# Projection to FFN: the last two units taken row block by row block, one normalisation factor per row block, constant products on TensorE, and the first chunk pair cast from a copy

## The reference, cut to what matters

```python
y = o.transpose(1, 0, 2, 3, 4).reshape(bn, n, d) @ w_o          # attention output projection
x = x + g1 * y                                                   # gated residual
hf = modulate(rms_norm(x, norm_ffn_g[i]), sh2, sc2)              # x * rsqrt(mean(x*x)+eps) * g, then (1+sc2), sh2
x = x + g2 * conv_ffn(hf, ffn_w_up[i], ffn_conv_w[i], ffn_conv_b[i], ffn_w_down[i])
```

## Time and profile before

| | |
|---|---|
| median of 3 runs | 2498.31 us (2495.0 to 2499.1) |
| profiled execution | 2497.54 us, span in the trace 2495.9 us |
| TensorE busy | 2469.8 us, 99% of the span |
| VectorE busy | 1788.2 us, 72% |
| ScalarE busy | 1185.5 us, 47% |
| GpSimd busy | 219.5 us, 9% |
| mean granted TensorE clock | 0.998 |

### The profile page before, as it was taken

How to read it: one execution, slowest core, us unless ns; L and a number is a source line. 1 busy time by engine, 2 the same in 40 slices (tenths; PEclk the granted TensorE clock), 3 DMA queues, 4 the chain that set the end, 5 groups by cost and what they waited for, 6 DMA issues and landing times.

```text
span 2495.9 us, 39539 instructions
## 1 busy us (share of the span) xinstructions
PE 2469.8 (99%) x14106; PEld 2157.8 (86%) x14106; DVE 1788.2 (72%) x2211; ACT 1185.5 (47%) x1517; POOL 219.5 (9%) x251
## 2 busy tenths in 40 slices
PE   9998999999999999999999999999999999999999
PEld 8988988888888888889999999988788888888887
DVE  6655766888898887787777777776666656665676
ACT  4445555544534535555333333344655435553463
POOL 5000000000000000222111111130200000000000
PEclk9999999999999999999999999999999999999999
DMA  8654586887787787775666656666566665566655
GB/s 269 182 133 110 153 282 204 273 298 243 258 275 247 240 288 246 251 221 167 198 188 186 195 183 198 185 217 191 179 188 193 193 194 178 185 198 194 185 176 173
DMA packets 279544, 519.07 MB, mean 208 GB/s; under 512 B 32750, under 2 KB 102648, under 8 KB 278672
## 3 DMA queue, kind: packets, MB, share of 16 engines
q1 hardware_dynamic: 254128, 403.66, 51.4%
q0 software_dynamic: 25120, 113.89, 14.7%
q10 hardware_dynamic: 192, 0.05, 0.0%
HBM read 515.35 MB, written 6.90 MB: 209 GB/s over the span
## 4 chain that ended last, share of the span: by engine, by line
PE 92%; DVE 3%; ACT 2%; DMA 2%; issue 1%; DVEq 0%; ACTq 0%
PE ps L1944 32%; PE ps L1971 22%; PE ps L1974 11%; PE ps L2452 7%; PE ps L2440 6%; PE ps L2445 4%; PE ps L1936 3%; PE ps L2394 1%; PE ps L2372 1%; DMA raw<-in_w_in 1%; DVE wlo L1199 1%; PE ps L2343 1%; DMA raw<-in_w_out 1%; PE ps L2261 1%; PE ps L2381 1%
## 5 line engine op out<-in xcount | busy, mean ns | idle before, releaser
L1199 DVE TENSOR_TENSOR wlo<-raw,whi 128x1024 fp32r<-128x1024 f32 (+1 forms) x776 | 943.9, 1228 | 424.0 <-ACT whi L706 407.3
L706 ACT ACTIVATE whi<-raw 128x1024 fp32r<-128x1024 f32 (+1 forms) x776 | 800.7, 1040 | 805.5 <-PE ps L1944 366.9
L1944 PE MATMUL ps<-whi,act 128*128 128x512 f32 (+3 forms) x2736 | 823.4, 382 | 1.9 <-DVE wlo L1199 1.2
L1971 PE MATMUL ps<-act,whi 128*128 128x512 f32 x2400 | 658.0, 395 | 1.7 <-DVE wlo L1199 1.4
L1944 PEld LDWEIGHTS ps<-whi,act 128*128 128x128 f32 x2736 | 505.4, 188 | 94.0 <-issue 3.2
L1944 PE MATMUL ps<-wlo,act 128*128 128x512 f32 (+3 forms) x1368 | 519.9, 380 | 0.0
L1971 PEld LDWEIGHTS ps<-act,whi 128*128 128x128 f32 x2400 | 410.2, 189 | 57.3 <-DVE wlo L1199 1.8
L1974 PEld LDWEIGHTS ps<-act,wlo 128*128 128x128 f32 x2400 | 369.5, 189 | 51.7
L1974 PE MATMUL ps<-act,wlo 128*128 128x256 f32 x2400 | 383.9, 281 | 0.0
L1944 PEld LDWEIGHTS ps<-wlo,act 128*128 128x128 f32 x1368 | 257.4, 188 | 45.0
L1525 DVE SCALAR_TENSOR_TENSOR arena<-arena,cond 128x768 f32<-128x768 f32 (+1 forms) x330 | 285.6, 888 | 5.9 <-DMA arena<-in_w_ada 2.6
(11 more groups left out here) (327 smaller groups left out, 2140.4 us busy)
## 6 DMA issues: line engine op xcount, KB each, us to landing
arena<-in_w_ada POOLq DMA_DIRECT2D x128, 768.0 KB, 5.8
raw<-in_ffn_w_up SPq DMA_DIRECT2D x160, 512.0 KB, 4.3
raw<-in_w_mlp_in SPq DMA_DIRECT2D x128, 512.0 KB, 4.8
raw<-in_w_mlp_out SPq DMA_DIRECT2D x128, 512.0 KB, 5.1
raw<-in_na_w_qkv SPq DMA_DIRECT2D x96, 512.0 KB, 4.8
raw<-in_ffn_w_down SPq DMA_DIRECT2D x84, 512.0 KB, 4.4
raw<-in_w_in SPq DMA_DIRECT2D x64, 384.0 KB, 3.7
raw<-in_w_in SPq DMA_DIRECT2D x32, 512.0 KB, 4.4
```

Of the source, the lines that this page charges most:

```text
L706: act.activation(a, b, ACT.Copy).then_inc(hi_done, 1)
L1199: dve.tensor_tensor(a, b, c, ALU.subtract).then_inc(lo_done, 1)
L1944: ins = pe.matmul(o, a, b, start=start and i == 0, stop=last and i == 2, skip_group_check=True)
L1971: pe.matmul(Z[q][:, c, :].rearrange("p (h t) -> p h t", h=2), kn(whi, j)[:, kk, P * c:P * c + P], act2[:, :, k, 0:S], start=k == 0, stop=k ...
```

## The change

On TensorE the last two units of the projection's last panel run together in `last_units`: first all products of row block 0 (which then counts up `wo_half`), then those of row block 1; both units are counted in `unit_used` at the end. VectorE adds row block 0, sums its squares, adds row block 1, squares it itself with a reducing product and sums again; ScalarE has one logarithm and exponential per row block, and all four scalings of row block 0 between the two. TensorE turns pairs 0 to 3 of row block 0 first, then issues four products of constants into `G[0]`, then turns row block 1. For pair 0 VectorE writes `turned_f` straight from the transposes, ScalarE casts `ahi` from that copy, and VectorE subtracts, chunk by chunk.

```diff
 ScalarE
-            for r in range(RT):
-                act.wait_ge(x4_ok, 4 + r)
-                own.done(act.activation(junk_w, x[:, r, 1536:D], ACT.Square, accum_out=psq[:, r, 3:4]))
+            act.wait_ge(x4_ok, 4)
+            own.done(act.activation(junk_w, x[:, 0, 1536:D], ACT.Square, accum_out=psq[:, 0, 3:4]))
             act.sem_inc(psq2_ok, 1)
-            act.wait_ge(mean_ok, 1)
-            own.done(act.activation(frms[:, 1, :], frms[:, 0, :], ACT.Ln, scale=1.0 / D, bias=EPS))
-            act.activation(frms[:, 1, :], frms[:, 1, :], ACT.Exp, scale=-0.5).then_inc(rms_ok, 1)
+            def row_rms(r):
+                act.wait_ge(mean_ok, r + 1)
+                own.done(act.activation(frms[:, 1, r:r + 1], frms[:, 0, r:r + 1], ACT.Ln, scale=1.0 / D, bias=EPS))
+                act.activation(frms[:, 1, r:r + 1], frms[:, 1, r:r + 1], ACT.Exp, scale=-0.5).then_inc(rms_ok, 1)
+            row_rms(0)
             act.wait_ge(rms_ok, 1)
+            for c in range(4):
+                scale_piece(c, xs, x, frms[:, 1, 0:1])
+            row_rms(1)
             act.wait_ge(coef_ok, 3)
...
-            scale_piece(0, xs, x, frms[:, 1, 0:1])
-            scale_piece(1, xs, x, frms[:, 1, 0:1])
-            turn(5, 0, g_ffn, b_ffn, at_=(0, 1))
-            scale_piece(2, xs, x, frms[:, 1, 0:1])
-            turn(5, 0, g_ffn, b_ffn, at_=(2,))
-            scale_piece(3, xs, x, frms[:, 1, 0:1])
-            turn(5, 0, g_ffn, b_ffn, at_=(3,))
+            for c in range(2):
+                act.wait_ge(a_f, 2 * KC + c + 1)
+                act.activation(ahi[:, c, 0:S], turned_f[:, 0, c, :], ACT.Copy).then_inc(a_hi, 1)
+            turn(5, 0, g_ffn, b_ffn, at_=range(1, 4))
             split(U_FFN, 3)
 VectorE
-            def turn(e, off, gain, shift=None, order=range(8), at_=range(8)):
+            def turn(e, off, gain, shift=None, order=range(8), at_=range(8), early=False):
                 for at in at_:
-                    dve.wait_ge(a_hi, TURN_AT[e] + 2 * at + 2)
+                    if early:
+                        dve.wait_ge(turned, 8 * e + at + 1)
+                    else:
+                        dve.wait_ge(a_hi, TURN_AT[e] + 2 * at + 2)
...
+            def add_last_row(r, ready):
+                dve.wait_ge(*ready)
+                v, y = x[:, r, 1536:D], tmp[:, 512 * r:512 * r + 512]
+                own.done(dve.tensor_tensor(y, G[1][:, r, :], gb[:, 1536:D], ALU.mult))
+                dve.tensor_tensor(v, v, y, ALU.add).then_inc(x4_ok, 1)
+            def row_mean(r):
+                dve.tensor_reduce(frms[:, 0, r:r + 1], psq[:, r, :], AXX, ALU.add).then_inc(mean_ok, 1)
...
-            add_last(1, U_WO + 32, drained[1])
+            add_last_row(0, (wo_half, 1))
             dve.wait_ge(psq2_ok, 1)
-            dve.tensor_reduce(frms[:, 0, :], psq[:, :, :], AXX, ALU.add).then_inc(mean_ok, 1)
-            dve.wait_ge(rms_ok, 1)
+            row_mean(0)
+            add_last_row(1, (unit_used, U_WO + 32))
+            dve.sem_inc(drained[1], 1)
+            dve.wait_ge(x4_ok, 5)
+            own.done(dve.tensor_tensor_reduce(tmp[:, 0:512], x[:, 1, 1536:D], x[:, 1, 1536:D], 1.0, 0.0, ALU.mult, ALU.add,
+                                              psq[:, 1, 3:4]))
+            row_mean(1)
+            dve.wait_ge(rms_ok, 2)
...
-            turn(5, 0, g_ffn, b_ffn, at_=(0,))
-            dve.wait_ge(a_f, 2 * KC + 2)
-            dve.tensor_tensor(alo[:, 0:2, 0:S], turned_f[:, 0], f(ahi[:, 0:2, 0:S]), ALU.subtract).then_inc(a_lo, 2)
+            turn(5, 0, g_ffn, b_ffn, at_=(0,), early=True)
+            for c in range(2):
+                dve.wait_ge(a_hi, TURN_AT[5] + c + 1)
+                dve.tensor_tensor(alo[:, c, 0:S], turned_f[:, 0, c, :], f(ahi[:, c, 0:S]), ALU.subtract).then_inc(a_lo, 1)
             turn(5, 0, g_ffn, b_ffn, at_=(1,))
 TensorE
-            def last_units(u0, parts, acc, t0, final):
+            def last_units(u0, parts, acc, t0, final, half):
                 pe.wait_ge(lo_done, u0 + parts[-1][0] + 1)
                 for r in range(RT):
...
                     if r == 0:
-                        ins.then_inc(half_rows, 1)
+                        ins.then_inc(half, 1)
                 ins.then_inc(unit_used, len(parts))
...
+                    if n == 3 and j >= 6:
+                        if j == 7:
+                            last_units(U_WO, ((30, 12, 2), (31, 14, 2)), G[1], S, KC - 1, wo_half)
+                        continue
                     unit_rows(U_WO, 8 * n + j, q, 2 * j, S)
...
+            def ffn_first_steps():
+                for r, scaled in enumerate((xs_a, xs_v)):
+                    for at in range(4):
+                        pe.wait_ge(scaled, 4 + at // 2 + 1)
+                        for c in range(2):
+                            k = 2 * at + c
+                            ins = pe.transpose(X[at][:, c * S + P * r:c * S + P * r + P], xs[:, r, P * k:P * k + P], ident)
+                        if r == 1:
+                            ins.then_inc(turned, 1)
+                    if r == 0:
+                        for _ in range(4):
+                            pe.matmul(G[0][:, 0, 0:S], ident, cst[:, 0:S], start=True, stop=True)
...
-                                ffn_steps(((0, 1, 2, 3), (4,), (5,), (6, 7))[j])
+                                if j == 0:
+                                    ffn_first_steps()
+                                else:
+                                    ffn_steps(((4,), (5,), (6, 7))[j - 1])
```

More of the change, by code:

```diff
@@ L344, in program @@
         xs_a, xs_v = sem("xs_a"), sem("xs_v")
-        x4_ok, psq2_ok, mean_ok, rms_ok = (sem("ffn_" + n) for n in ("x", "sq", "mean", "rms"))
+        x4_ok, psq2_ok, mean_ok, rms_ok, wo_half = (sem("ffn_" + n) for n in ("x", "sq", "mean", "rms", "half_rows"))
         hid_a, hid_v = sem("hid_a"), sem("hid_v")
@@ L2528, in _ @@
                         if j == 5:
-                            last_units(U_DOWN, ((21, 6, 2), (22, 8, 2), (23, 10, 1)), GD[1], S, 10)
+                            last_units(U_DOWN, ((21, 6, 2), (22, 8, 2), (23, 10, 1)), GD[1], S, 10, half_rows)
                     else:
```

## The result

The changed kernel takes 2501.23 us in the median of 22 runs, the kernel before 2497.28 us in 22 runs beside them (the three runs shown ahead had 2498.31).

The account below looks back on a forecast made before the run. TensorE, busy 2469.8 of 2495.9 us, bounds the kernel; only its 9.09 us seam between projection and FFN counts. FFN shift 4.1 plus stall 0.1 makes 4.2 us on 2497.54: 2501.7 us, range 2498.0 to 2505.0.

Parts of the forecast that it names:

- Head start: Row block 0, done 2.72 us ahead, gains nothing: unit 34's split waits ahead of it; its scaling comes 1.11 us later.
- Constant products: Four float32 products on TensorE ahead of row block 1's transposes: end at 1772.7, last 2.2 us on the path.
- The bounds: On TensorE, the constant products take 1.71 us at the upper clock, 3.41 us at the lower.
- case C: Constant products on TensorE cost nothing: FFN's first product 2.1 us later than before, time 2499.6 us; chance 0.09.
- Pair 0: Between transposes and the FFN's first product, pair 0 itself is faster by 1.6 us than the old way.
- Unit 1: In the FFN, TensorE may wait for GpSimd's low part of pair 1: 0 to 0.9 us, by the median 0.1.
- Slow start: FFN's first four products took 1.33 us instead of 1.09 before; starting at full clock takes 0.24 off the shift.
- A: TensorE's clock returns late, slowing constant products and pair 0's transposes: 5.2 to 5.3 us in all, 2502.8 us; chance 0.30.
- B: Row block 0's early finish is real, unit 34's split released at 1759.15: -0.4 to +1.8 us, 2497.1 to 2499.3; chance 0.06.

Follow-up runs that it names:

- units in order: Changed kernel with the projection's last two units run unit by unit, each counted at its end: ratio 1.0011 to the kernel before, seam 10.28 us.
- old pair 0: Changed kernel with pair 0 of the FFN's input made as in the kernel before: one execution only, no ratio, seam 13.67 us.
- each unit counted: Changed kernel with unit 30 counted behind its own last product, order and work unchanged: ratio 1.0014 to the kernel before, seam 11.88 us.
- eight products: Changed kernel with eight constant products instead of four: one execution only, no ratio, seam 15.38 us.
- no products: Changed kernel without its four constant products: ratio 1.0021 to the kernel before, seam 11.47 us.
- shortened seam: Changed kernel with unit 34's split moved behind the second logarithm (ScalarE) and ahead of the FFN's next split (VectorE): ratio 0.9994; also without constant products, 1.0001.

## Why the prediction was right

2501.7 us was forecast with 4.2 us more than the profile before; the seam grew by 4.23, and the median by 4 us. The mechanism was right in both costs, the late split and the uncovered products. That the seam is met to 0.03 us is luck: it hangs on the clock's return, which came 4.37 us after the first transpose as in the kernel before, but after 2.9 to 5.0 in the experiments that kept the products and a late first transpose, and that moves the seam by up to 0.75 us.

**Head start.** Lost as forecast, by the split of unit 34. Gate product forecast 2.37 behind the projection's end, found 2.34; first transposes 6.17 forecast and found. Counting unit 30 sooner brought the gate product 1.3 us forward, moving the split out of the way 4.8 us.

**Constant products.** Forecast to end 10.95 behind the end and to leave some 2.2 us uncovered; row block 1's transposes started 10.94 behind it, 2.2 after their piece was ready. The bounds, 1.71 and 3.41 us, hold: the eight rows ran 3.03 from their first start to the next transpose. That row block 1 does not pass them is what the Trainium skill, "TensorE: Matmul & The Clock Gate", section "Step-by-step", says of program order, and the trace agrees by that 2.2 us.

**What the products give.** Here a term was mis-sized. The prediction put the upper clock at the FFN's start at 0.24 us, from how the kernel before started. Without the products the clock came back 4.7 us later after the first transpose than in the kernel before, and the FFN's start lost 1.69 us. That kernel has 16 transposes in a row, the changed one without products eight, a gap of 0.66 us and eight more; that this is what kept the clock down is argued here, and not tried apart. So taking the products out could not have given case C's 2499.6. The Trainium skill, "TensorE: Matmul & The Clock Gate", says in "What's actually happening" that the clock is halved by default and activity releases it; the traces agree, with a return 9.0 us after the first transpose without the products and 2.9 to 5.0 with them. That the products would cost nothing, as the prediction read out of that rule, the runs do not bear out: they cost 1.85 us and give back 1.69.

**Pair 0.** Here, too, a size was off: forecast 1.6 us, found 1.0: the 4.03 of before held two transposes more, at the lower clock, which the copy has no part in. The forecast 2.46 from the first transpose to the FFN (0.41 and 2.05) was right, 2.38.

**Unit 1.** A stall of 0 to 0.9, taken at 0.1; found none: unit 1 starts 3.27 behind the first product, 3.40 before.

**Slow start.** 0.24 was taken off for the FFN's start at the upper clock; its first four products took 1.19 instead of 1.33, so 0.14 was gained. The 1.09 of the forecast is a later row; the row that comes behind transposes takes 1.17 at the upper clock in the kernel before, too. This error and that on unit 1 cancel.

**Rivals.** A needed a return 5.6 us after the first transpose; it came after 4.37. B was wrong for this kernel, and right for the one with the split out of the way, where the gain is larger than B's best, since B left the split ahead of row block 0. C fell with the 2.2 us uncovered; its own terms put the FFN's start 2.1 to 2.4 us later, of which it took the lower end.

## What to carry to other kernels

Where work is reordered so that a part is done early, look first at what stands ahead of its consumer in that engine's own order, and at which count releases that: two units counted together free the first one's buffer only when the second is done. Filler products on TensorE belong where TensorE provably waits for something later; ahead of work that gets ready meanwhile they are paid for in full (2.06 us for four more here), and only a clock that comes back sooner sets something against it (1.69 us for the first four, which cost 1.85). What the clock is worth is read in a run without the filler, not in a kernel whose gap looks different.

## What was not expected

The time from TensorE's first transpose behind the gap to the full clock varied between profiles, though all but the kernel before run the same transposes and products behind that gap: 4.37 us in both the kernel before and the changed one, 2.9 with the units in order, 3.0 with the old pair 0, 4.2 with each unit counted, 5.0 with eight products. That alone moves the seam by up to 0.75 us (four constant products of 2.45 to 3.20 us). The clock's fall varied as well: it came 2.2 (each unit counted) to 5.0 us (no products) behind the projection's end, with TensorE idle from that end on in all of them. In the shortened seam's profiles the clock stayed up with the products, TensorE idle for 1.65 us ahead of the transposes and 1.34 us ahead of the FFN; without them it fell, although TensorE had stood idle only for 1.74 and 1.42 us, with eight transposes (1.18 us) between.
